# Three of six gate tiles move from the attention stage to the end of the input stage

## The reference, cut to what matters

```python
p = h @ lp['w_in']        # [RWKV r|k|v|loras, q | k | v, gate_a, gate_b]
...
merged = jax.nn.sigmoid(p[..., OFF_GA:OFF_GB]) * y_a \
       + jax.nn.sigmoid(p[..., OFF_GB:D_IN]) * y_b
return merged @ lp['w_o'], ...
```

## Time and profile before

| | us |
|---|---|
| median of three runs | 4147.22 |
| lowest to highest | 4144.95 to 4151.42 |
| profiled execution, its own time | 4154.28 |
| profiled execution, span of the trace | 4152.5 |
| input stage, turn of pair 3 (TensorE, last two small products and VectorE's chain) | 318.4 to 348.8 |
| scan stage, first instruction of POOL | 353.85 |
| attention, first to last product of its side tiles | 1052.1 to 1231.1 |

### The profile page before, as it was taken

The page is one execution under the profiler, slowest core; times in us unless marked ns, Lnnn a source line. Parts: engine busy times, 40 slices in busy tenths (PEclk is TensorE's granted clock), DMA queues, the critical chain, the costliest instruction groups (busy, mean ns, idle before and its releaser), DMA issues. The chain is left out here.

```text
span 4152.5 us, 58569 instructions
## 1 busy us (share of the span) xinstructions
PE 3510.3 (85%) x22502; PEld 2528.0 (61%) x22502; DVE 2448.4 (59%) x5167; ACT 950.5 (23%) x1414; POOL 1496.8 (36%) x1269
## 2 busy tenths in 40 slices
PE   5996999976887998988889999885877777878997
PEld 3664666653655788767676676654555455545656
DVE  3364222235213441999989999996766666664445
ACT  2121111112221232322222232222111111112122
POOL 0001111100002002144465565656666656664530
PEclk8998999987888999999999999997999899999999
DMA  5100111015004124688899999999999999999992
GB/s 193 36 21 17 33 32 34 31 48 222 25 31 194 51 77 129 201 297 285 293 353 356 344 393 354 347 319 342 388 389 397 376 396 394 380 388 389 394 339 90
DMA packets 365007, 973.66 MB, mean 234 GB/s; under 512 B 35937, under 2 KB 133417, under 8 KB 355776
## 3 DMA queue, kind: packets, MB, share of 16 engines
q0 software_dynamic: 150912, 549.52, 34.9%
q1 hardware_dynamic: 213824, 420.38, 28.6%
HBM read 863.22 MB, written 106.55 MB: 234 GB/s over the span
## 5 line engine op out<-in xcount | busy, mean ns | idle before, releaser
L1945 POOL DMA_INDIRECT u_rows<-in_u_rows,idx_u x512 | 674.2, 1317 | 785.7 <-DVE dots L1983 580.4
L1956 POOL DMA_INDIRECT v_rows<-in_v,idx_v x512 | 637.5, 1245 | 254.5 <-issue 145.8
L1983 DVE CUSTOM_DVE_ANT_0 u_rows<-u_rows,x_rows 128x1024 f32<-128x1024 f32 x512 | 619.4, 1221 | 147.2 <-DMA u_rows<-in_u_rows,idx_u 113.6
L2393 PE MATMUL hid_ps<-dh,u_high 128*128 128x512 f32 x1152 | 475.6, 413 | 78.7 <-DVE u_low L2645 43.3
L2393 PE MATMUL hid_ps<-dl,u_high 128*128 128x512 f32 x1152 | 471.3, 409 | 0.0
L2393 PE MATMUL hid_ps<-dh,u_low 128*128 128x512 f32 x1152 | 469.4, 407 | 0.0
L2042 PE MATMUL ff_ps<-v_rows,diag 128*8 128x512 f32 x2048 | 265.6, 639 | 74.1 <-DMA v_rows<-in_v,idx_v 70.7
L2393 PEld LDWEIGHTS hid_ps<-dh,u_high 128*128 128x128 f32 x1152 | 225.5, 196 | 144.6 <-DVE u_low L2645 67.1
L2851 ACT ACTIVATE dh<-v_raw 128x1024 fp32r<-128x1024 f32 x128 | 135.3, 1057 | 737.3 <-DMA v_raw<-in_v 571.3
L2906 PE MATMUL turn_ps<-w_high,dh 128*128 128x512 f32 x384 | 169.9, 443 | 148.4 <-DVEq L2988 112.0
L671 PE MATMUL side_ps_scan<-h,w_side_scan 128*128 128x344 f32 x768 | 269.5, 477 | 0.3
(11 more groups left out here) (440 smaller groups left out, 6454.0 us busy)
## 6 DMA issues: line engine op xcount, KB each, us to landing
u_raw<-in_u SPq DMA_DIRECT2D x128, 512.0 KB, 6.3
v_raw<-in_v SPq DMA_DIRECT2D x128, 512.0 KB, 12.9
hidden_saved<-hid SPq DMA_DIRECT2D x128, 256.0 KB, 7.1
gates_saved<-gates SPq DMA_DIRECT2D x32, 1024.0 KB, 7.9
hidden_back<-hidden_saved SPq DMA_DIRECT2D x128, 256.0 KB, 13.7
g_back<-gates_saved SPq DMA_DIRECT2D x60, 320.0 KB, 16.3
x<-in_w_ada SPq DMA_DIRECT2D x16, 1024.0 KB, 7.9
g_back<-gates_saved SPq DMA_DIRECT2D x30, 384.0 KB, 21.1
```

What stands on the lines that cost most here:

```text
L1945: self.nc.gpsimd.indirect_dma_start(self.u[:, n % RU], None, self.io["u_rows"], bass.IndirectOffsetOnAxis(ap=index, axis=axis)).then_inc(l ...
L1956: self.nc.gpsimd.indirect_dma_start(self.v[:, n % RV], None, self.io["v"], bass.IndirectOffsetOnAxis(ap=index, axis=0)).then_inc(self.v_la ...
L1983: V.tensor_tensor_reduce(self.u[:, n % RU], self.u[:, n % RU], self.xt[:], 1.0, 0.0, ALU.mult, ALU.add, accum_out=self.dots[:, i % 2, k:k ...
L2393: mm = nc.tensor.matmul(ps[b % 2][:], u[:, b % RING, k], h[:, k], start=at == 0, stop=at == 3 * KD - 1)
```

## The change

Side tiles 19, 20 and 21 (three gate tiles) leave the attention stage and join the list of the input stage in the turn of pair 3, in the places that the next pair's tiles have in the other turns. `SIDE_AT_INPUT` is 19. The input stage loads their weights into the same three places, ScalarE copies each whole tile into `raw[0]`, whose last reader is pair 2, after a wait for `turn_done` of three pairs, and SP stores each to `side_saved`. SP's store of the shifted rows now waits for the last mix of a tile and not for the end of the last turn. In the attention stage three tiles are left; the loop still has three turns of two bodies, and the first body of each carries a tile. The rest of the diff passes the tile's number in place of a flag, gives VectorE's loop the same count, and adds one semaphore. Cut to its core:

```diff
+SIDE = 6 + 2 * KD
+SIDE_MOVED = 3
+SIDE_AT_INPUT = SIDE - SIDE_MOVED
...
             if p + 1 < NP:
                 uses.append(("in", FIRST + 3 * (p + 1) + q))
+            else:
+                uses.append(("side", q))
             if name:
                 uses.append((name, p))
...
             @block.sync
...
-                    sp.dma_start(w[:, n % 3], io["w_in"][n]).then_inc(w_loaded[n % 3], 16)
+                    block = io["w_in"][n] if n < COUNT else io["w_side"][SIDE_AT_INPUT + n - COUNT]
+                    sp.dma_start(w[:, n % 3], block).then_inc(w_loaded[n % 3], 16)
...
-                for n in range(3, COUNT):
+                for n in range(3, COUNT + SIDE_MOVED):
                     load(n)
-                sp.wait_ge(turn_done, NP)
+                sp.wait_ge(mixed, COUNT)
                 sp.dma_start(io["shift_out"], last[:]).then_inc(out_done, 16)
+                for q in range(SIDE_MOVED):
+                    sp.wait_ge(taken, evicted["side", q])
+                    sp.dma_start(io["side_saved"][:, SIDE_AT_INPUT + q, :], raw[0][q][:, 1:]).then_inc(side_stored, 16)
                 sp.wait_ge(out_done, 16)
+                sp.wait_ge(side_stored, 16 * SIDE_MOVED)
...
             @block.tensor
...
-                    if what == "in":
+                    if what in ("in", "side"):
+                        if what == "side":
+                            n += COUNT
                         pe.wait_ge(w_loaded[n % 3], 16 * (n // 3 + 1))
...
             @block.scalar
...
+                    elif what == "side":
+                        act.wait_ge(turn_done, NP - 1)
+                        S.activation(tiles(raw[0][n][:, 1:]), src, ACT.Copy).then_inc(taken, 1)
                     elif what == "decay":
...
 def attention(nc, io, sb, pb, sm, consts, x, h, ob, **_):
...
-            LEFT = SIDE - NC
+            LEFT = SIDE_AT_INPUT - NC
...
-                    body(0, 0, False)
-                    with eng.Fori(0, LEFT // 2) as i:
+                    body(0, 0, None)
+                    with eng.Fori(0, LEFT) as i:
                         for q in range(2):
-                            body(i * 2 + (q + 1), 1 - q, True)
-                    body(NB - 1, 1, False)
+                            body(i * 2 + (q + 1), 1 - q, None if q else i)
+                    body(NB - 1, 1, None)
...
                 @block.tensor
...
-                            if beside:
-                                side.multiply(pe, b - 1, range(*products))
+                            if beside is not None:
+                                side.multiply(pe, beside, range(*products))
...
                 @block.scalar
...
-                        for t in range(2 if beside else 0):
-                            side.take(act, b - 1, t)
+                        for t in range(0 if beside is None else 2):
+                            side.take(act, beside, t)
...
-                        if beside:
-                            side.take(act, b - 1, 2)
+                        if beside is not None:
+                            side.take(act, beside, 2)
```

More of the change, by code:

```diff
@@ L450, in rwkv_inputs @@
         (lora_loaded, small_loaded, w0_loaded, w1_loaded, w2_loaded, projected, summed, taken, mixed, tanh_ready, sq_ready, rk_ready,
-         scan_ready, exp_ready, exp_used, bonus_taken, turn_done, edges_ready, chain, out_done) = sems(
+         scan_ready, exp_ready, exp_used, bonus_taken, turn_done, edges_ready, chain, out_done, side_stored) = sems(
             ph, "lora_loaded", "in_small_loaded", "w0_loaded", "w1_loaded", "w2_loaded", "projected", "in_summed", "taken", "mixed",
             "tanh_ready", "sq_ready", "rk_ready", "scan_ready", "exp_ready", "exp_used", "bonus_taken", "turn_done", "edges_ready",
-            "in_chain", "shift_stored")
+            "in_chain", "shift_stored", "side_stored_in")
         w_loaded = (w0_loaded, w1_loaded, w2_loaded)
@@ L625, in _ @@
                     dve.sem_inc(turn_done, 1)
-SIDE = 6 + 2 * KD
 class Side:
@@ L1326, in _ @@
                     bias_and_max(0, 0, True)
-                    body(0, 0, False)
-                    with dve.Fori(0, LEFT // 2) as i:
+                    body(0, 0, None)
+                    with dve.Fori(0, LEFT) as i:
                         link.enter(i, 12)
                         for q in range(2):
-                            body(i * 2 + (q + 1), 1 - q, True)
-                        link.leave(LEFT // 2)
-                    body(NB - 1, 1, False)
+                            body(i * 2 + (q + 1), 1 - q, None)
+                        link.leave(LEFT)
+                    body(NB - 1, 1, None)
         with ExitStack() as ph:
```

## The result

The changed kernel takes 4127.69 us (median of five runs, 4122.81 to 4138.53) where the kernel before takes 4147.22 (4144.95 to 4154.12): a ratio of 0.9949, 95% interval 0.9932 to 0.9967, 19.5 us faster. The forecast was 4115.7, 12.0 us lower; the range of 4096 to 4133 holds the result, the narrower own range of 4110 to 4121 does not.

The account below looks back on a forecast made before the run. TensorE was taken to set the pace in attention, waiting 22.9 us for tile weights. Input stage +20.1 and attention -51.6 gave -31.5 us, from 4147.2 to 4115.7; range 4096 to 4133.

Parts of the forecast that it names:

- the narrower own range: Whole kernel: 4110 to 4121 us, from the store's bounds and where the clock falls in unfilled attention bodies.
- the rival of the half clock: Attention: unfilled bodies at half clock from their first score, 16.1 us more in all, 4131.8 us; chance 0.12.
- The input stage: Input stage with three tiles added: next stage begins 20.1 us later (17.3 to 21.5).
- The order of pair 2: Input stage's last turn: pair 3 follows pair 2's interleaved order, moved by 50.02 us; third tile's eviction ends at 365.98.
- the third tile's store: End of input stage: 516 KB store taken as 4.4 us, between 1.6 and 5.8, added to 3.44 us without store.
- Attention: Attention with three tiles fewer: 139.8 us in place of 191.4, saving 51.6; filled body 25.99, unfilled 15.53.
- the first rival: Attention: TensorE keeps full clock throughout, some 18.4 us more saved, 4097 us; chance 0.11.
- Full clock throughout: Attention: without weight waits, products with v take 3.79 us in unfilled bodies; 4097 us in all; chance 0.11.
- Half clock from the first score: Attention: unfilled bodies slow from their scores on, 5.35 us more each, 4131.8 us in all; chance 0.12.
- The input stage hides nothing: Input stage: three tiles add all their TensorE time, 45.2 us with the store; 4140.8 us; chance 0.06.
- Attention loses its full clock: Attention: filled bodies also at 1.2 GHz, 218.0 us in place of 191.4; 4194 us in all; chance 0.05.

Follow-up runs that it names:

- the changed kernel with 40 products ahead: Changed kernel plus 40 unread 8-column TensorE products ahead of the input stage's first product: 4130.95 us, ratio 0.9950 to the kernel before.
- the input stage alone: Kernel before with the change's input stage, attention still computing all six tiles: 4173.98 us, ratio 1.0075.

## Why the prediction was right, and where it was off

The range holds the result, but the middle of it was missed by 12.0 us, and by the number alone the rival of the half clock (4131.8) lies nearer than the forecast (4115.7). The traces refute that rival. The two stages came out as reasoned, and what is missing lies elsewhere; that the range is wide enough for it is owed to the room that was left for that rival, and so is luck.

**The input stage** came out as reasoned: +18.3 for +20.1. The order of pair 2 was the right pattern: the third tile's eviction ended 47.68 us after the start of the rate's (364.25 - 316.57), and pair 2 gave 315.96 - 268.27 = 47.69. VectorE's idle time ahead of the square root was 10.46 for 10.88; the weight loads cost nothing; the small store left the end. The term that was mis-sized is the third tile's store: from its issue to the next stage's first copy it takes 6.11 us (370.39 - 364.28), where 3.44 + 4.4 = 7.84 was taken. Less the 3.44, that is 2.7 in place of 4.4, and the row of these stores says 2.6. The prediction took the value between two other stores; the lower end, 1.6, was the nearer.

**Attention** gave 54.05 for 51.6. The pair took 41.03 for 41.52, from two errors that offset each other: the filled body's first twelve products took 4.65 where 5.4 was taken, and the unfilled body's products with v took 6.79 where body 7 had given 6.25. The filled body was 0.8 us shorter than taken, the unfilled one (1096.99 to 1112.84) 0.3 longer. Body 7 took 14.25 (1194.91 to 1209.16) for 15.21: after an unfilled body only its first transposes were slow throughout, the second group was back at 1.10. The forecast's picture held in each unfilled body of this trace: full clock in scores and transposes, half of it inside the products with v.

What it was read from was a lucky trace, though. The prediction took the fall of the clock from body 7 of the kernel before (6.25). In the five other traces with the attention stage of the kernel before, body 7's products with v took 3.79, behind the same two waits. And in the changed kernel with 40 products ahead, the first unfilled body kept the full clock too (granted 1.00, and 3.73 us for the next twelve tile products). TensorE's timeline, body 7 of the kernel before, run again, and that unfilled body:

```profile
1237.30 3.79 PE L1253 MATMUL o_ps<-vs,prob_t 128*128 128x64 f32 x32 [1.11 <-ACT prob_t L1284]
...
1111.69 3.79 PE L1270 MATMUL o_ps<-vs,prob_t 128*128 128x64 f32 x32 [1.11 <-ACT prob_t L1301]
```

In the other 17 of the 18 unfilled bodies, in the six traces with the attention stage of the change, the products with v took 5.47 to 6.87, so that what was assumed came true. But from another execution of the same kernel the first rival would have been read out of body 7. The same instructions with the same waits ran at either level; what decides between them stays open. The fall in the first trace also makes the 54.05 large: from the second one, 188.7 us, the change saves 51.4 for the 51.6 of the forecast.

**The rivals.** *Full clock throughout* would have shown 3.79 there, as one unfilled body of the 18 did. *Half clock from the first score* would have shown scores of 5.6; they took 2.96. *The input stage hides nothing* is refuted by the input stage alone (+18.3, not 45). *Attention loses its full clock* would have shown slow products in the middle of a filled body; its products with v took 3.79. The rule of the Trainium skill that was weighed, in "TensorE: Matmul & The Clock Gate", section "Loop structure matters more than you think", has a loop in which an engine copies a result away and the next products follow immediately, and says that the copy doesn't break the clock. In the unfilled bodies the products don't follow immediately: TensorE waits 1.11 us for ScalarE's copies, and the granted clock was 0.52 within the products behind: 6.79 us for 3.79. So in 17 unfilled bodies of 18 the rule could not be carried over to a copy that is waited for; in the eighteenth, and in body 7 of five of the six traces with the attention stage of the kernel before, the clock stayed at its full level.

**The later stages** are where the 12 us went that the forecast is too low. Its own two stages gave 4.2 us more than it had (1.8 and 2.4). Two sentences of it failed. The first is that a stage moves everything behind it by its own change in time, and, in its last part, that nothing in the diff reaches the stages beyond the merge: from the merge stage to the end the changed kernel took 8.0 us more than the profiled execution of the kernel before, and the stretches between the edited stages and the start made up 1.2 (+2.0 + 1.2 - 0.3 of the first table, less 1.7 by which the last turn of the input stage began earlier). The second is that the 7.1 us by which that execution lies above its median (4154.28 less 4147.22) carry over: that of the changed kernel lies on its own median. 8.0 + 1.2 - 4.2 + 7.1 = 12.1, the 12.0 but for rounding.

The two are partly one. Beside the second trace of the kernel before, whose execution lies on its median, the first one is 2.7 us longer in attention and 4.9 from the merge stage on. With the second trace in its place the sum by stages is simpler: +17.6 us to the scan's first copy, -0.1 in the scan, -51.4 in attention (137.35 for 188.7), -0.3 up to the merge stage and +12.9 from there to the end, in all -21.2 for the 19.5 and 20.6 of the medians. So the two edited stages were right to some 2 us, and nearly all that is missing lies behind the merge stage's first load. In single traces 13 us may still hold some scatter (above); the medians of two series say that some 12 are missing.

That the change's own work makes the later stages longer is not supported: the kernel before, with nothing but 40 hidden products added, takes 2885 there (and its median stays at 4149, since its scan is 6 to 8 shorter), the changed one with 20 takes 2878, and with 40 in both kernels the changed one is the shorter. With the same products in both, the change is worth 32.2 and 30.0 us, near the 31.5 of the forecast. So a shift of TensorE's program is enough for a difference of this size. That the change's shift is what made it here is the likeliest reading, and not shown: the change alters the programs of the other engines too, and only TensorE's was shifted by itself.

## What to carry to other kernels

Where an engine's program is long, an edit also moves all code behind it, and stages that it does not touch can change their length: a sum over stages of this kernel is good to some 10 us, and 20 tiny products cost it 30; the edit measured with such products in different numbers, in both kernels alike, tells it from its place (20, 32 and 30 us here). A clock that was seen to fall in one trace should be compared with a second one of the same kernel before a forecast rests on it. A wait for weights can be taken away as well by a second buffer as by moving the work (0.9933 and 0.9949 here, with intervals that overlap), and work that fills gaps is worth most spread over all of them: half a tile in each body gave 0.9877 where a whole one in every second gave 0.9949.

## What the runs showed that was not expected

- The length of the scan stage changes with what stands ahead of it in TensorE's program, and not in proportion: 541 to 543, 546 to 553 or 572 to 573 us for 40, 0 or 20 added products, in two kernels, with the time in every second turn of its loop; the change itself puts 72 products ahead of it and leaves it at 548 to 556.
- Six loads of weights in sequence with the products cost attention 26 to 30 us, more than the 22.9 us of the waits themselves: with two buffers the first twelve products of a body also take 3.74 us in place of 5.43.
- The same products with v, behind the same two waits of 1.1 us, take 3.79 us in one execution and 6.25 or more in another of the same kernel; with tile products in the waits' place they took 3.68 in all six bodies, and the clock granted over a whole pair is 1.00.
